# First modulation of a decoder block summed in parts of 4, 2 and 2 k-tiles, with low parts of its first weights on GpSimd

## What is computed

```
c_act = silu(c)
mod = c_act @ w_ada + b_ada                    # 1024 x 6144
sh1, sc1, gt1, sh2, sc2, gt2 = split(mod, 6)
h = rmsnorm(x, g_norm1) * (1 + sc1) + sh1      # "first modulation"
a_q, a_kv, i_q, i_k, i_w, b_*, c_*, z_* = split_cols(h @ w_in)
... branch A: an indexer scores the keys, top 128 kept, attention on them
... branch B: differential attention (its lambda from four vectors)
... branch C: dilated attention; gates, w_out, SwiGLU, last rmsnorm
```

## Time and profile before

| | |
|---|---|
| median of 3 runs | 1002.81 us (1002.26 to 1003.08) |
| the profiled execution's own time | 1003.18 us |
| its span on the core | 1001.4 us |
| TensorE (PE) busy | 984.4 us, 98% of the span |
| VectorE (DVE), ScalarE (ACT), GpSimd (POOL) busy | 481.1, 378.6 and 102.5 us |
| TensorE's granted clock over the span | 0.998 |

### The profile page before, as it was taken

How to read it: one execution, slowest core, us unless ns; L and a number is a source line. 1 busy time by engine, 2 the same in 40 slices (tenths; PEclk the granted TensorE clock), 3 DMA queues, 4 the chain that set the end, 5 groups by cost and what they waited for, 6 DMA issues and landing times.

```text
span 1001.4 us, 12705 instructions
## 1 busy us (share of the span) xinstructions
PE 984.4 (98%) x4925; PEld 805.3 (80%) x4925; DVE 481.1 (48%) x827; ACT 378.6 (38%) x679; POOL 102.5 (10%) x137
## 2 busy tenths in 40 slices
PE   7999999999999999999999999999999999999997
PEld 5778888878878767788788888988888888888886
DVE  4754777832244445564655563643433333331324
ACT  5345422254466666443223233542322322221222
POOL 1500000000064612200000002000000000000401
PEclk9999999999999999999999999999999999999999
DMA  8884226312131201255555642123344334222312
GB/s 329 261 267 140 85 84 174 99 43 85 63 108 32 64 23 32 74 197 174 182 183 204 221 153 84 63 84 105 108 142 153 120 105 147 84 105 84 126 43 84
DMA packets 88163, 123.13 MB, mean 123 GB/s; under 512 B 4824, under 2 KB 69941, under 8 KB 87986
## 3 DMA queue, kind: packets, MB, share of 16 engines
q1 hardware_dynamic: 87442, 115.98, 35.4%
q0 software_dynamic: 528, 6.22, 2.1%
q10 hardware_dynamic: 144, 0.26, 0.1%
HBM read 119.77 MB, written 8.45 MB: 128 GB/s over the span
## 4 chain that ended last, share of the span: by engine, by line
PE 91%; DMA 3%; DVE 2%; issue 2%; ACT 1%; POOL 1%; SPq 0%; POOLq 0%; DVEq 0%; ACTq 0%
PE tile_ps L859 18%; PE tile_ps L861 18%; PE tile_ps L860 18%; DMA w_raw<-in_w_in_dram 2%; PE t_ps L1125 2%; PE s_ps L1107 2%; PE o_ps L1154 2%; PE tile_ps L1303 1%; PE s_ps L1304 1%; PE s_ps L1303 1%; PE t_ps L1304 1%; PE t_ps L1303 1%; PE tile_ps L1302 1%; PE tile_ps L1304 1%; PE s_ps L1302 1%
## 5 line engine op out<-in xcount | busy, mean ns | idle before, releaser
L859 PE MATMUL tile_ps<-h_hi,w_hi 128*128 128x512 f32 x736 | 291.4, 396 | 1.6 <-DVE w_lo L1814 1.0
L860 PE MATMUL tile_ps<-h_lo,w_hi 128*128 128x512 f32 x736 | 286.9, 390 | 0.0
L861 PE MATMUL tile_ps<-h_hi,w_lo 128*128 128x512 f32 x736 | 286.8, 390 | 0.0
L1814 DVE TENSOR_TENSOR w_lo<-w_raw,w_hi 128x2048 fp32r<-128x2048 f32 (+3 forms) x60 | 131.3, 2189 | 162.1 <-ACT w_hi L1428 162.1
L859 PEld LDWEIGHTS tile_ps<-h_hi,w_hi 128*128 128x128 f32 x736 | 138.1, 188 | 38.9 <-issue 8.2
L861 PEld LDWEIGHTS tile_ps<-h_hi,w_lo 128*128 128x128 f32 x736 | 138.2, 188 | 29.4
L860 PEld LDWEIGHTS tile_ps<-h_lo,w_hi 128*128 128x128 f32 x736 | 138.3, 188 | 27.4 <-issue 0.2
L1428 ACT ACTIVATE w_hi<-w_raw 128x2048 fp32r<-128x2048 f32 (+3 forms) x60 | 107.3, 1788 | 42.7 <-PE tile_ps L861 9.1
L1811 DVE TENSOR_TENSOR t_lo<-t_raw,t_hi 128x2048 fp32r<-128x2048 f32 (+1 forms) x15 | 32.8, 2184 | 85.6 <-ACT t_hi L1426 85.5
L1426 ACT ACTIVATE t_hi<-t_raw 128x2048 fp32r<-128x2048 f32 (+1 forms) x15 | 27.0, 1799 | 81.5 <-PE s_ps L1304 53.5
L1573 ACT ACTIVATE nl<-nl,cst 128x256 f32<-128x256 f32 (+3 forms) x81 | 42.8, 529 | 35.8 <-DVE cst L2023 35.3
(11 more groups left out here) (404 smaller groups left out, 1680.8 us busy)
## 6 DMA issues: line engine op xcount, KB each, us to landing
w_raw<-in_w_in_dram SPq DMA_DIRECT2D x31, 1024.0 KB, 5.4
w_raw<-in_w_gate_up_dram SPq DMA_DIRECT2D x22, 1024.0 KB, 7.0
ada<-in_w_ada_dram SPq DMA_DIRECT2D x12, 1024.0 KB, 5.5
t_raw<-in_w_down_dram SPq DMA_DIRECT2D x10, 1024.0 KB, 5.0
row_copies<-row_flat POOLq DMA_DIRECT2D x1, 5632.0 KB, 21.5
ada<-in_w_ada_dram SPq DMA_DIRECT2D x8, 640.0 KB, 11.5
ada<-in_w_ada_dram SPq DMA_DIRECT2D x8, 512.0 KB, 4.3
ada<-in_w_ada_dram SPq DMA_DIRECT2D x8, 384.0 KB, 10.0
```

The lines of the kernel that those rows point to most:

```text
L859: pe.matmul(dst[0:mw, :], wh, x_hi[:, kx, :], start=start, stop=False)
L860: pe.matmul(dst[0:mw, :], wh, x_lo[:, kx, :], start=False, stop=False)
L861: mm = pe.matmul(dst[0:mw, :], wl, x_hi[:, kx, :], start=False, stop=stop)
L1814: dve.tensor_tensor(w_lo[s][:, 0:kt, 0:n_cols], w_raw[s][:, 0:kt, 0:n_cols], w_hi[s][:, 0:kt, 0:n_cols].bitcast(F32), ALU.subtract) \
```

## The change

- `FIRST_KTS` becomes kt 0 to 3, kt 4 and 5, kt 6 and 7. `N_DIRECT` is (2, 0, 0): parts 1 and 2 are added up wholly by DVE, as 1 scaling and 7 additions of 128x512 each. Part 0's tiles are 1024 columns instead of 1280, part 1's were 768. All sums in TensorE use 128 columns (`SUM_W` = 100 is gone).
- w_ada's part comes as 8 transfers of 512 KB and twice 8 of 256 KB, the last 8 issued after part 0's sums (`mod1_made`).
- The low parts of kt 4 to 7 of chunks 0 and 1 (`w_lo[n][:, 4:KT]`, 128x1024 each) are made by POOL, between the h tiles of kt 1 and 2 and those of kt 4 and 7. ACT makes h for kt 3 and 5, DVE for kt 0 and 6.
- TensorE's order: products of kt 0 to 3 (t 0, 1, 2 and half of t 3), sums of part 1, the rest of t 3, then kt 4 and 5, in the midst of them the sums of part 2, then kt 6 and 7.
- The first 128 columns of chunk 2 (the first key tile's weights) are split ahead of its other 72, and the product with them waits for them alone (`first_lo` 3). Lambda's small operations on DVE and ACT go behind `make_lo(4)` and `make_hi(4)`.
- POOL issues `power(2)` ahead of `row_copies`, and `row_copies` waits for the high part of chunk 4 (`w_hi_made[0]` at 3).
- In the loop over attention steps the reciprocals of two tiles are made together in odd steps ahead of the low part of the next chunk.

```diff
-FIRST_KTS = (range(0, 5), range(5, 8))
-SUM_W = 100
-N_DIRECT = (2, 1)
+FIRST_KTS = (range(0, 4), range(4, 6), range(6, 8))
+N_DIRECT = (2, 0, 0)
+N_ADDED = (0, 6, 14)
...
             for q, kts in enumerate(FIRST_KTS):
+                if q == 2:
+                    sp.wait_ge(mod1_made, 1)
                 for k in range(KT):
                     sp.dma_start(ada1[q][k][:], w_ada[k * P:(k + 1) * P, 0:2, kts[0] * P:(kts[-1] + 1) * P]) \
-                        .then_inc(ada1_in[q][k], 16)
+                        .then_inc(ada1_in[q % 2][k], 16)
...
+            sp.wait_ge(first_lo, 1)
             load(2, [(KT, 0, cols(COL_AKV, P)), (KT, P, cols(COL_IKW, 72))])
+            sp.wait_ge(first_lo, 2)
             load(3, [(KT, 0, cols(COL_AQ, CW))])
...
-            for kt in range(2, 5):
-                hidden_full(kt)
+            hidden_full(1)
+            hidden_full(2)
+            for n in range(2):
+                pool.wait_ge(w_hi_made[n], 1)
+                pool.tensor_tensor(w_lo[n][:, 4:KT, :], w_raw[n][:, 4:KT, :], w_hi[n][:, 4:KT, :].bitcast(F32),
+                                   ALU.subtract).then_inc(w_split[n], 1)
+            hidden_full(4)
+            hidden_full(7)
...
-            for kt in FIRST_KTS[1]:
-                hidden_full(kt)
+            power(2, rs_kv, ms_kv, 4)
             pool.wait_ge(rows_stored, 16 * 4)
-            pool.wait_ge(h_ready, KT)
+            pool.wait_ge(w_hi_made[0], 3)
             pool.dma_start(rep_dram, row_dram.to_broadcast([P, FL_W])).then_inc(rows_copied, 16)
-            power(2, rs_kv, ms_kv, 4)
...
+            def column_sums(q):
+
+                if N_DIRECT[q] == 0:
+                    pe.wait_ge(ada1_added, N_ADDED[q] + KT)
+                    add_up(q, 1)
+                    add_up(q, 0).then_inc(mod1_made, 1)
+                    return
...
             query_part(2, FIRST_KTS[0])
-            query_part(3, range(0, 4))
-            pe.wait_ge(ada1_added, 2 * KT - 3)
-            add_up(1, 0)
-            add_up(1, 1).then_inc(mod1_made, 1)
-            query_part(3, range(4, 5))
+            query_part(3, range(0, 2))
+            column_sums(1)
+            query_part(3, range(2, 4))
             chunk_ready(0)
...
+            query_part(2, FIRST_KTS[1])
+            column_sums(2)
+            query_part(3, FIRST_KTS[1])
...
             for t in range(2, 4):
-                query_part(t, FIRST_KTS[1])
+                query_part(t, FIRST_KTS[2])
+            pe.wait_ge(first_lo, 3)
+            project(0, 4, h_hi, h_lo, straight, 0, bank=key_ps[0])
             s = chunk_ready(2)
-            project(s, 4, h_hi, h_lo, straight, 0, bank=key_ps[0])
...
             add_part(0, range(2, KT))
             amplitude(0)
...
-            lo_part(1, 0, first_hi, 2, first_lo)
-            add_part(1, range(1, 5))
-            lo_part(0, 1, w_hi_made[0], 1, w_split[0])
-            add_part(1, range(5, KT))
-            lo_part(1, 1, w_hi_made[1], 1, w_split[1])
+            full_here(0)
+            lo_part(0, 0, 4, first_hi, 1, first_lo)
+            hidden_lo(0)
+            hidden_lo(1)
+            add_part(1, range(0, 1))
+            hidden_lo(2)
+            hidden_lo(3)
+            lo_part(1, 0, 4, first_hi, 2, first_lo)
+            add_part(1, range(1, KT))
+            add_part(2, range(0, 2))
             amplitude(1)
+            add_part(2, range(2, 3))
             for kt in FIRST_KTS[1]:
                 hidden_lo(kt)
+            add_part(2, range(3, KT))
+            amplitude(2)
...
             for v in range(N_STEP):
-                if v % 2 == 0 and v < MIX_B:
-                    reciprocal(v - 1)
                 for u in steps_begun_at(v):
                     shift(subs_of(u)[0])
-                if v % 2 or v == MIX_B:
-                    reciprocal(v - 1)
+                if v % 2:
+                    for u in (v - 1, v):
+                        reciprocal(u)
                 if v < MIX_B and lo_at(v) is not None:
                     make_lo(lo_at(v))
```

More of the change, by code:

```diff
@@ L901, in direct @@
                 n = len(FIRST_KTS[q])
-                dst, w = (sum_ps, SUM_W) if q == 0 else (last_ps, P)
-                pe.wait_ge(ada1_in[q][k], 16)
+                wait_ada1(pe, q, k)
                 for g in gs:
                     for m in range(n):
-                        pe.matmul(dst[g][:, m, :], ada1[q][k][:, g, m * P:(m + 1) * P],
-                                  c_act[:, k:k + 1].to_broadcast([P, w]), start=k == 0 and m == 0,
+                        pe.matmul(sum_ps[q][g][:, m, :], ada1[q][k][:, g, m * P:(m + 1) * P],
+                                  c_act[:, k:k + 1].to_broadcast([P, P]), start=k == 0 and m == 0,
                                   stop=last and m == n - 1)
@@ L930, in add_up @@
                 n = len(FIRST_KTS[q])
-                dst, w = (sum_ps, SUM_W) if q == 0 else (last_ps, P)
                 for m in range(n):
-                    mm = pe.matmul(dst[g][:, m, :], ada1_sum[q][:, g, m * P:(m + 1) * P], ones[:, 0:w],
-                                   start=False, stop=last and m == n - 1)
+                    mm = pe.matmul(sum_ps[q][g][:, m, :], ada1_sum[q][:, g, m * P:(m + 1) * P], ones[:],
+                                   start=N_DIRECT[q] == 0 and m == 0, stop=last and m == n - 1)
                 return mm
@@ L970, in _ @@
                 turn_x(kt)
+            def column_sums(q):
[4 more added lines that the diff above has]
+                    return
+                pe.wait_ge(ada1_added, N_ADDED[q] + KT - 1 - N_DIRECT[q])
+                add_up(q, 1, last=False)
+                direct(q, KT - 1, gs=(1,), last=True)
+                pe.wait_ge(ada1_added, N_ADDED[q] + KT - N_DIRECT[q])
+                add_up(q, 0).then_inc(mod1_made, 1)
             pe.wait_ge(xt_read, 1)
             keep_busy(2)
[L973 to L977 removed]
+            column_sums(0)
             keep_busy(2)
             pe.wait_ge(first_hi, 1)
[L980 removed]
+            for kt in FIRST_KTS[0]:
                 hi_hi(kt)
             pe.wait_ge(first_lo, 1)
[L983 to L986 removed]
+            for kt in FIRST_KTS[0]:
                 hi_lo(kt)
@@ L1503, in _ @@
             make_hi(4, 5)
+            act.wait_ge(lam_dot, 1)
+            act.activation(lam_e, lam_s, ACT.Exp).then_inc(lam_exped, 1)
             def index_relu(n):
@@ L1880, in _ @@
+            dve.wait_ge(xt_read, 1)
             dve.wait_ge(amp_ready, 1)
[L1881 to L1888 removed]
@@ L1892, in _, with query_lo @@
             amplitude(1)
+            add_part(2, range(2, 3))
             for kt in FIRST_KTS[1]:
                 hidden_lo(kt)
+            add_part(2, range(3, KT))
+            amplitude(2)
+            dve.wait_ge(xt_read, 7)
+            dve.wait_ge(amp_ready, 3)
+            full_here(6)
+            for kt in FIRST_KTS[2]:
+                hidden_lo(kt)
+            def query_lo(t):
+                dve.wait_ge(iq_hi_made, t + 1)
+                for h, (d0, d1) in ((2 * t, (0, DH)), (2 * t + 1, (DH, 0))):
+                    ins = dve.tensor_tensor(iq_split[d1:d1 + DH, h, :], query_ps[t][d0:d0 + DH, :],
+                                            iq_split[d0:d0 + DH, h, :].bitcast(F32), ALU.subtract)
+                ins.then_inc(tile_out[t % 2], 1)
@@ new lines, in _ @@
+            dve.wait_ge(first_hi, 3)
+            dve.tensor_tensor(w_lo[0][:, :, 0:P], w_raw[0][:, :, 0:P], w_hi[0][:, :, 0:P].bitcast(F32), ALU.subtract) \
+                .then_inc(first_lo, 1)
+            dve.wait_ge(w_hi_made[0], 2)
+            dve.tensor_tensor(w_lo[0][:, :, P:P + 72], w_raw[0][:, :, P:P + 72], w_hi[0][:, :, P:P + 72].bitcast(F32),
+                              ALU.subtract).then_inc(w_split[0], 1)
+            for t in (0, 1, 2, 3):
+                query_lo(t)
+            make_lo(3)
@@ L1895, in _ @@
+            dve.wait_ge(ik_hi_made, 1)
+            for d1 in (0, DH):
+                ins = dve.tensor_tensor(ik_lo[d1:d1 + DH, :], key_ps[1][0:DH, :], ik_hi[0:DH, :].bitcast(F32),
+                                        ALU.subtract)
+            ins.then_inc(tile_out[1], 1)
+            make_lo(4)
             dve.wait_ge(small_in, 16 * 5)
```

124 lines of the change are left out of this document (51 added, 73 removed).

## The result

| | before | after |
|---|---|---|
| median of 6 runs each | 1003.09 us (1002.26 to 1003.95) | 1006.92 us (1005.84 to 1007.78) |
| ratio, 95% interval | | 1.0034 [1.0024, 1.0044] |
| span of the profiled execution | 1001.4 us | 1004.4 us |
| PE's granted clock over the span | 0.998 | 0.996 |

What follows compares the result with a forecast made beforehand. TensorE, busy 984.4 of 1001.4 us, was taken as the bound, through its waits and slow start. Start stage +4.1, row copies -1.2, reciprocals -1.1 gave +1.8 on 1002.81: 1004.6 us, range 999.9 to 1007.2.

Steps and rivals of the forecast that it cites:

- (A): Low parts on GpSimd stop VectorE's additions in the start stage; 1004.6 us, range 1003.2 to 1006.4, chance 0.58.
- (B): Additions and GpSimd don't stop each other, or only in gaps; 1000.1 us, range 999.3 to 1001.6, chance 0.27.
- (C): As (A), but low parts or h of kt 4 come late, or copies delay chunk 8; 1006.6 us, chance 0.15.
- signs of being wrong: Additions share the ports, the stall of (c) or (d) only moves, or PE's clock stays low beyond eight passes.
- (d): Attention loop: reciprocals made earlier in pairs remove PE's 0.9 us wait for POOL's tile at 327 us: -1.1 us.
- (a): Start stage: fewer TensorE passes ahead of the first product of h, which comes 1.9 us sooner.
- (b): Start stage, additions of parts 1 and 2: chunk 2 0.4 us sooner without GpSimd, 3.7 us later with it.
- GpSimd's stop: Start stage: GpSimd's two subtractions stop VectorE's additions for 4.2 us; bounds none and 4.7 us.
- The clock: Start stage: eight passes may run slowly behind PE's wait of 5 us; 0.4 us, bounds 0 and 0.8.
- (c): Mid-kernel: moved row copies let chunk 4's weights land sooner, so PE's wait for the low part goes: -1.2 us.
- Cost nil: Moved row copies meet chunk 8's load; its landing 1.2 us later is covered by 6.0 us.
- up to 0.5 if it lands at 129.8: Upper bound on the moved row copies' cost: up to 0.5 us if chunk 8's load lands at 129.8 us.

Runs made afterwards that it cites:

- the first two experiments: Changed kernel with low parts back on VectorE: ratio 1.0017 to before; changed kernel with ScalarE copying raw weights instead, subtraction left out: ratio 0.9977.

## Why the prediction came out as it did

**The likeliest case (A) was right in kind:** two-operand subtractions on GpSimd stop VectorE's additions, chunk 2 comes 4.3 us later (forecast 4.1), and a part is won back. Rival (B), additions unharmed, falls with the first two experiments and the two stretched additions. The size was not (A)'s: 1006.92 lies above its own range, 1003.2 to 1006.4, and inside that of (C), 1005.1 to 1008.5. Yet neither stall that (C) names came about: h of kt 4 didn't wait for GpSimd's low parts, and chunk 8 still lands in time. Of the prediction's own signs of being wrong, two came true, a stall in (d) that only moved and a clock low for longer than eight passes. By the Trainium skill, page "SBUF — State Buffer", section "SBUF: two separate sides", the lock covers an operation of VectorE with two inputs in SBUF; the trace agrees for GpSimd's subtractions, 2.88 and 2.70 us for additions of 0.75. It doesn't agree with a lock held for GpSimd's whole instruction where that reads one operand: there two additions lost 0.77 and 0.59 us, and one of 0.75 ran inside GpSimd's operation.

**(a) First product sooner.** Forecast -1.9 us, measured -2.60 between the two profiles (28.99 to 26.39). The term was sized too small, but a part of it is chance: of the passes at 0.21 us there are 26 in the trace of before and 16 in that of after, where the prediction took 27 and 29. Ten fewer are 10 x 0.10 = 1.0 us of which it had none. The 32 passes began at 12.43, not 0.3 us sooner: the smaller first transfer brought nothing.

**(b) VectorE's queue.** Without GpSimd, 29.3 us from amplitudes to chunk 2 were forecast (27.1 to 56.4) and 29.70 measured. GpSimd's stop: 4.2 forecast, 4.09 measured. The clock: 0.4 forecast for eight passes, 0.9 measured on the path. PE stayed slow for the 8 passes and 6 products behind, of which the latter were covered by the wait for part 2. Together 34.70 against the 33.8 of the forecast (27.1 to 56.76 + 4.1): the terms mis-sized are the clock, by 0.5, and VectorE's own queue, by 0.4.

**(c) Row copies.** -1.2 forecast, -1.38 measured alone. "Cost nil" for chunk 8 held, with less to spare than reckoned: the load was 24.3 us on the way, not 21, and 4.1 of the 6.0 us of cover were used, not 1.2. The bound "up to 0.5 if it lands at 129.8" doesn't follow from the prediction's own rows: 129.8 + 1.9 + 2.3 is 134.0, when PE takes it.

**(d) Reciprocals, the step that failed.** The prediction took "the whole" of 1.1 us since "the loop is regular and shows no other such stall"; 0.08 was won. Its bounds included 0, but for the wrong reason: the stall didn't move to a low part on VectorE, it uncovered ScalarE's eviction, due 0.05 us before PE went on. That could have been read in the trace of before, 0.7 us behind the row of the wait.

The sum: -0.7 in (a), +0.9 in (b), +1.0 in (c) and (d) together (-1.33 for -2.3) make the +3.0 of the profiled spans out of the +1.8 forecast. The first of these errors hid part of the others, so that the start stage came within 0.2 us of its forecast (4.32 for 4.1) partly by luck. The 0.8 us between the spans' 3.0 and the medians' 3.8 is not explained here.

## What to carry to other kernels

Work moved from VectorE to an idle GpSimd isn't free when both operate on two operands in SBUF: add nearly the whole working length of GpSimd's operation to VectorE's queue (here 2.05 us of stop for each 2.25), and compare it with VectorE's own price for the work (1.2). Before a wait is counted as won, look at what else the waiting engine needs at its next instruction, and when that was ready: only the distance to the second-latest is won. Where two engines share a reduction, balance it by the queue's end, not by the number of operations; an early start given to one is lost if the other ends the sum.
